# Two later layers: banded attention steps between the products of the projection tiles, norms applied behind the products, and half of the output projection inside the difference attention

## What is computed

```python
for l in range(DEPTH):
    h = rmsnorm_2(x, g_attn[l])
    proj = jnp.einsum('bsd,dc->bsc', h, w_in[l])
    qa, ka, va, qb, kb, vb = jnp.split(proj, offs, axis=-1)
    ...
    ya = windowed_gqa_sink(qa, ka, va, sink[l])
    yb = diff_attention(qb, kb, vb, lam)
    yb = rmsnorm_2(yb, subln[l]) * (1.0 - lambda_init)
    y = jnp.concatenate([ya.reshape(B, S, SWA_Q), yb.reshape(B, S, DIFF_V)], axis=-1)
    x = x + jnp.einsum('bsm,md->bsd', y, w_out[l])
    h = rmsnorm_2(x, g_ffn[l])
    gate, val = jnp.split(jnp.einsum('bsd,df->bsf', h, w_up[l]), 2, axis=-1)
    gate = centred_dwconv(gate, conv_w[l], conv_b[l])
    x = x + jnp.einsum('bsf,fd->bsd', jax.nn.silu(gate) * val, w_down[l])
```

## Time and profile before

| | |
|---|---|
| median of 3 runs | 3187.5 us (3186.05 to 3193.69) |
| the profiled execution | 3192.74 us |
| its span, first to last instruction | 3191.0 us |
| busy: TensorE, VectorE, ScalarE | 2972.4, 1523.6, 1190.8 us |
| mean granted TensorE clock | 0.972 of 2.4 GHz |
| the first later layer, from its norm to its end | 678.2 us (1830.3 to 2508.5) |
| the second | 679.5 us (2508.5 to 3188.0) |

### The profile page before, as it was taken

How to read it: one execution, slowest core, us unless ns; L and a number is a source line. 1 busy time by engine, 2 the same in 40 slices (tenths; PEclk the granted TensorE clock), 3 DMA queues, 4 the chain that set the end, 5 groups by cost and what they waited for, 6 DMA issues and landing times.

```text
span 3191.0 us, 36914 instructions
## 1 busy us (share of the span) xinstructions
PE 2972.4 (93%) x14632; PEld 2430.2 (76%) x14632; DVE 1523.6 (48%) x2217; ACT 1190.8 (37%) x1784; POOL 0.2 (0%) x4
## 2 busy tenths in 40 slices
PE   6999699999999889999999998789999997899999
PEld 4788588999999766557888776368888774478887
DVE  3121755552454444436636456855444457654343
ACT  3111543331332365334424344643233444543232
POOL 0000000000000000000000000000000000000000
PEclk9999899999999999999999999999999998999999
DMA  6665001221212111002322211012223220023223
GB/s 243 220 225 183 7 31 53 67 67 59 66 60 71 49 39 39 1 14 95 107 92 93 99 67 53 1 53 99 100 92 102 76 73 14 14 86 106 87 98 106
DMA packets 67276, 255.94 MB, mean 80 GB/s; under 512 B 7456, under 2 KB 11168, under 8 KB 66464
## 3 DMA queue, kind: packets, MB, share of 16 engines
q1 hardware_dynamic: 67104, 253.58, 23.1%
HBM read 251.46 MB, written 2.10 MB: 79 GB/s over the span
## 4 chain that ended last, share of the span: by engine, by line
PE 85%; DVE 6%; DMA 3%; ACT 3%; issue 3%; SPq 0%; DVEq 0%; ACTq 0%
PE psum L520 71%; DVE arena L1371 2%; ACT temps L1014 2%; DVE row_stats L1371 2%; DMA modulation_weights<-in_ada 2%; PE psum L837 2%; PE psum L856 1%; PE psum L834 1%; PE psum L559 1%; PE psum L977 1%; DMA arena<-in_ada_first 1%; PE psum L757 1%; PE psum L771 1%; PE psum L847 1%; DVE temps L1371 1%
## 5 line engine op out<-in xcount | busy, mean ns | idle before, releaser
L520 PE MATMUL psum<-arena_r,w_hi 128*128 128x512 f32 (+1 forms) x7640 | 2077.3, 371 | 42.3 <-DVE arena_r L1371 38.8
L520 PEld LDWEIGHTS psum<-arena_r,w_hi 128*128 128x128 f32 x7640 | 1404.0, 189 | 254.4 <-issue 78.0
L520 PE MATMUL psum<-arena_r,w_lo 128*128 128x512 f32 (+1 forms) x3820 | 1264.6, 367 | 0.0
L1371 DVE TENSOR_TENSOR w_lo<-w_raw,w_hi 128x1024 fp32r<-128x1024 f32 (+3 forms) x367 | 453.9, 1237 | 768.8 <-ACT w_hi L1014 768.7
L520 PEld LDWEIGHTS psum<-arena_r,w_lo 128*128 128x128 f32 x3820 | 709.4, 189 | 84.9
L1014 ACT ACTIVATE w_hi<-w_raw 128x1024 fp32r<-128x1024 f32 (+3 forms) x367 | 391.7, 1067 | 829.6 <-DMA w_raw<-in_weights 829.4
L1371 DVE SCALAR_TENSOR_TENSOR temps<-psum,vectors,temps 128x511 f32<-128x511 f32 x352 | 228.0, 679 | 150.4 <-ACT temps L1014 147.3
L1014 ACT ACTIVATE temps<-psum,vectors 128x512 f32<-128x512 f32 (+1 forms) x132 | 112.2, 850 | 179.8 <-PE psum L520 178.4
L1014 ACT ACTIVATE arena<-psum 128x768 f32<-128x768 f32 (+1 forms) x134 | 96.6, 727 | 155.3 <-PE psum L520 63.7
L1014 ACT ACTIVATE temps<-temps 128x512 f32<-128x512 f32 (+2 forms) x165 | 108.3, 656 | 90.6 <-DVE temps L1371 88.6
L1014 ACT ACTIVATE temps<-psum 128x512 f32<-128x512 f32 (+1 forms) x142 | 86.9, 655 | 145.6 <-PE psum L520 123.8
(11 more groups left out here) (147 smaller groups left out, 1850.9 us busy)
## 6 DMA issues: line engine op xcount, KB each, us to landing
w_raw<-in_weights SPq DMA_DIRECT2D x275, 512.0 KB, 3.2
w_raw<-in_weights SPq DMA_DIRECT2D x64, 704.0 KB, 4.0
temps<-in_ada SPq DMA_DIRECT2D x40, 512.0 KB, 3.6
modulation_weights<-in_ada SPq DMA_DIRECT2D x40, 512.0 KB, 4.4
arena<-in_ada_first SPq DMA_DIRECT2D x4, 2048.0 KB, 23.7
X<-in_xt SPq DMA_DIRECT2D x1, 3072.0 KB, 12.6
phase_constants<-in_const SPq DMA_DIRECT2D x3, 768.0 KB, 7.4
w_raw<-in_weights SPq DMA_DIRECT2D x12, 192.0 KB, 2.3
```

Of the source, the lines that this page charges most:

```text
L520: last = mm(lin_at(t, segs, slots, upper)[:, s:s + m], w[:, c], x(k, s, m), start=(k == 0 and a == 0), stop=(k == n_k - 1 and a == 2))
L1371: op(*args, **kw).then_inc(*C.out(signal))
```

## The change

Four things, in both later layers.

**The factor of the norm is applied behind the products.** The products take X times the gain, as it is (`raw_hi` by ScalarE, `raw_low` by VectorE, made while the residual is added); the sums of squares come between blocks 3 and 4 of the first tile; each result is then multiplied by 1/rms on VectorE: all 18 projection tiles (`scaled`), the 22 gate tiles, and the 22 products of gate and value.

**Banded steps inside the projection.** Tiles 9 to 17 carry two steps each, cut in between their blocks. The order of TensorE's banks changes: linear tiles have two banks instead of four, tails and rotations share bank 0, banded scores have one pair of banks, turned ones another.

**Turning by a product.** Instead of dividing the 512 or 768 exponentials by their sum and transposing, VectorE writes a diagonal matrix of the two heads' reciprocals (`SHARE`), and an ordinary fp32 product with it both turns and divides.

**Half of the output projection inside the difference attention.** The tiles of w_out are cut into two halves of 4 blocks; the first half, which needs the banded heads alone, runs as 8 tiles of 12 products between the 16 steps, and is added to X there (8 more additions). The turned blocks have one bank instead of two, and values and sum of squares share bank 2. The second half follows as 8 tiles of 12 products.

```diff
-        t += [(8, P, lambda g, l=l, c=m * P: columns(paired_rows(g["w_out_2"][l]), c)) for m in range(8)]
+        for part in range(2):
+            t += [(4, P, lambda g, l=l, r=part * 512, c=m * P: columns(paired_rows(g["w_out_2"][l])[r:r + 512], c)) for m in range(8)]
...
+        BAND = 9
+        def band_step(n):
+            return 2 * (n - BAND) if BAND <= n < 18 else None
...
+                if raw:
+                    linear(1, segs, hi, lo, "free_v", 4, progress("raw_done", 8), between=lambda k: norm_sum(segs) if k == 3 else None)
+                else:
+                    norm_sum(segs)
+                    linear(2, segs, hi, lo, "free_v", 4, progress("h_done", 8))
...
+                def tail(n):
+                    pe.wait_ge(sems["free_a"], first + n + 1)
+                    if n:
+                        taken_from(n - 1)
+                    wait(pe, C.at("rot_done", on="rope_made"))
+                    if specs[n]["kind"] == "norm":
+                        last = mm(PS[:, 0, :], blk, T[:, n % 2, 0:NX], start=True, stop=True)
+                    else:
+                        for t in range(4):
+                            last = pe.transpose(PS[:, 0, t * P:(t + 1) * P], T[:, n % 2, t * P:(t + 1) * P], ident)
+                    last.then_inc(*C.out("tail_sum"))
...
+                def rotation(n, latest):
+                    if n < 0 or specs[n].get("rope") is None:
+                        return
+                    pe.wait_ge(sems["tail_made"], tails + n + 1)
+                    taken_from(latest)
+                    wait(pe, C.at("rot_done", on="rope_made"))
+                    mm(PS[:, 0, :], CP[:, PC_ROT:PC_ROT + P], f_(specs[n]["rope"], NX), start=True, stop=True).then_inc(*C.out("rot_done"))
...
-                            last = pe.transpose(PS[:, hf, t * P:(t + 1) * P], f_(a, P), ident)
+                            last = mm(PS[:, 6 + hf, t * P:(t + 1) * P], f_(a, P), SHARE[n % 2][:, hf], start=True, stop=True)
...
+                def between(n):
+                    p = band_step(n)
+                    def at(k):
+                        if n == 0 and k == 3:
+                            sums()
+                        if p is not None:
+                            if k == 0:
+                                scores(p)
+                            if k == 2:
+                                turn(p - 1)
+                            if k == 4:
+                                values(p - 2)
+                                scores(p + 1)
+                        if n and k == (3 if p is None else 5):
+                            tail(n - 1)
+                        if p is not None:
+                            if k == 6:
+                                turn(p)
+                            if k == 7:
+                                values(p - 1)
+                        if k == 7:
+                            rotation(n - 3, n - 1)
+                    return at
...
+                ready = progress("raw_done", 8)
+                for n in range(18):
+                    linear(1, ONLY_X, raw_hi, raw_lo, "free_a", 2, ready if n == 0 else None, between(n), t0)
...
-                    if n >= 2:
-                        pe.wait_ge(sems["pt_made"], base + n - 1)
+                    if n:
+                        pe.wait_ge(sems["pt_made"], base + n)
+                    else:
+                        taken_from(17)
...
-                        last = pe.transpose(PS[:, n % 2, t * P:(t + 1) * P], f_(E2 + n % 4 * 1024 + t * P, P), ident)
+                        last = pe.transpose(PS[:, 0, t * P:(t + 1) * P], f_(E2 + n % 4 * 1024 + t * P, P), ident)
...
-                        pe.wait_ge(*C.at("od_made"))
+                        pe.wait_ge(*C.at("sub_rs"))
...
+                for m in range(8):
+                    linear(1, ONLY_X, hi2, lo2, "free_v", 2, ready if m == 0 else None,
+                           lambda k: difference(2 * m + k // 2) if k % 2 else None, t0)
...
+            def raw_low(m, gain):
+                dve.wait_ge(*C.next("raw_hi"))
+                step(stt, "raw_done", r_(RAW0 + 8 * NX + m * NX, NX), X[:, m, 0:NX], gain(m), r_(RAW0 + m * NX, NX).bitcast(F32),
+                     ALU.mult, ALU.subtract)
...
+                        if raw and part == 0:
+                            dve.wait_ge(*C.at("lin_done"))
+                            src = SCALED[i % 2]
+                            step(tt, "raw_scaled", halves(src), halves(lin_at(t, segs, 4)), RS, ALU.mult)
...
+                    if raw:
+                        step(tt, "prod_made", halves(T[:, 3, 0:NX]), halves(T[:, 3, 0:NX]), RS, ALU.mult, after=C.at("free_v"))
...
-                    step(tt, "p_made", e, e, ST[:, s + 12:s + 14].rearrange("p (h o) -> p h o", o=1).broadcast_to([P, 2, w]), ALU.mult,
-                         after=C.at("dve_own"))
+                    step(tt, "p_made", SHARE[n % 2], CF[:, C_ID:C_ID + P].rearrange("p (o q) -> p o q", o=1).broadcast_to([P, 2, P]),
+                         ST[:, s + 12:s + 14].rearrange("p (h o) -> p h o", o=1).broadcast_to([P, 2, P]), ALU.mult, after=C.at("dve_own"))
...
+                for n in range(1, 19):
+                    p = band_step(n)
+                    scaled(n - 1)
+                    if p:
+                        probs(p - 1)
+                    if p is not None and p < 16:
+                        maxima(p)
+                    if p is not None and p >= 6 and p % 4 == 2:
+                        low((p - 6) // 4)
+                    if n < 18:
+                        ahead()
+                    if n >= 2 and (specs[n - 2]["kind"] == "norm" or n < BAND + 1):
+                        tail(n - 2)
+                    if n >= 4 and specs[n - 4].get("rope") is not None:
+                        rotate(specs[n - 4]["rope"], PS[:, 0, :])
+                    if p is not None and p < 16:
+                        probs(p)
+                    if n >= BAND and specs[n - 1]["kind"] != "norm":
+                        tail(n - 1)
+                    if p is not None and p + 1 < 16:
+                        maxima(p + 1)
...
+                    if n % 2 == 0:
+                        t = ahead()
+                        dve.wait_ge(*C.at("lin_done"))
+                        x = X[:, n // 2, 0:NX]
+                        step(tt, "free_v", x, lin_at(t, ONLY_X, 2, t0), x, ALU.add)
```

267 lines of the change are left out of this document (166 added, 101 removed).

## The result

The changed kernel takes 3216.65 us (median of 4 runs, 3215.71 to 3221.45), beside 3188.2 us for the kernel before: a ratio of 1.0081, 95% interval 1.0067 to 1.0095. It is **slower by 0.8%**. The forecast of 3192.5 us was 24 us low, and its most likely case, no change, did not come; the time that came is close to the third rival's 3214 us. The first later layer now takes 691.7 us (678.2 before). Two such layers give 27.0 us, and the medians lie 28.5 apart. The spans of the two profiled executions (3215.1 us against 3191.0) differ by less, since the first later layer begins 3.0 us sooner in the second (1827.3 against 1830.3) and the one before was 5 us above its median.

What follows compares the result with a forecast made beforehand. TensorE was taken to bound the kernel (85% of the chain of waits). Per layer -15.4 - 27.4 + 10.4 + 33 + 2 + 15.4 - 15.5 = +2.5, both layers +5: 3187.5 + 5 = 3192.5 us, range 3152 to 3222.

Steps and rivals of the forecast that it cites:

- most likely case, no change: Whole kernel: large terms nearly cancel, time within 9.6 us of 3187.5; chance 0.40.
- third rival: Difference attention hides nothing and its clock sinks: 10.6 us more per layer, 3214 us; chance 0.27.
- Norms: At the norms, gaps and slow clock go while the sums stay: -15.4 us per layer.
- the remaining half: Output projection's second half: VectorE and ScalarE set 3.2 us per tile; with the net's start, -15.5 us per layer.
- the start of the net: Feed-forward net's first tile: norm sum waits 2.8 us; counted within the remaining half's -15.5 us per layer.
- Tail and rotation in one bank: Projection tiles 4 to 8: TensorE waits 4.6 us five times, plus 10 for slow clock: +33 us per layer.
- 0, if the wait were covered: Lower bound of the cost of tail and rotation sharing one bank; the upper bound was 41 us.
- first rival: Tiles 4 to 8: the wait for the rotation is covered, 33 us per layer go, 3126 us; chance 0.15.
- Turning by a product: Banded steps: 80 blocks at 0.27 us instead of a transpose's 0.14, +10.4 us per layer; keeping transposes 20.8 faster overall.
- Banded steps inside the tiles: Banded attention's 63.0 us stage goes, 35.6 us of TensorE work enters projection tiles: -27.4 us per layer.
- Difference attention: With half the output projection inside: 84.1 us against 68.7, +15.4 per layer, two thirds of the moved work not hidden.
- waits in the banded tiles: Tiles 9 to 16: rotation late by about 0.7 us in three tiles, +2 us per layer.

Runs made afterwards that it cites:

- experiment 1: The change with VectorE's w_lo subtraction moved behind tail and rotation in tiles 4 to 8: 3148.8 us, ratio 0.9861 to the kernel before.
- experiment 3: The change with probabilities turned by transposes again and VectorE dividing all of them: 3211.7 us, ratio 1.0058 to the kernel before.
- experiment 5: The change with the output projection's first half run behind the difference attention instead of inside it: 3230.0 us, ratio 1.0117 to the kernel before.
- experiment 4: The change with the difference attention's addition to X moved into the odd step, behind its probabilities: 3204.9 us, ratio 1.0033 to the kernel before.
- experiment 7: The change with the difference attention's first maximum ahead of the last tail and last banded low half: 3214.4 us, ratio 1.0076 to the kernel before.
- experiments 5 and 6: The second of these is experiment 5's kernel with turned blocks going to two banks in turn: 3229.6 us, ratio 1.0116 to the kernel before.
- the run with all orders: The change with w_lo behind tail and rotation, both additions to X moved, transposes, and first maximum ahead of last tail: 3106.0 us, ratio 0.9730 to the kernel before.
- experiment 2: The change with unread products filling TensorE's waits in tiles 4, 5, 6 and 8 and before tile 6's rotation: 3203.1 us, ratio 1.0027.

## Why the prediction was right or wrong

Per layer the forecast was +2.5 us and the measurement is +13.5.

**Norms, the remaining half, the start of the net: right.** The gaps are gone. The second half of the projection runs at 3.28 us per tile (forecast 3.2), and the norm sum of the net waits 2.45 us (2.8). From the end of the difference attention to the end of the layer it is 390.2 us, against 413.2 before: -23.0, forecast -23.4.

**Tail and rotation in one bank: right, and it decides.** Five stalls, 25.4 us (forecast 23), and 10.5 for the clock behind them (10): 35.9 where the record has 33, and experiment 1 gets back all but the 1.4 us that it leaves. One of the five isn't where I put it: the tail of tile 7 doesn't wait. In its place it is the rotation in tile 6, for 6.17 us, because VectorE itself copies the value tile's turned blocks out of the bank, behind a `w_lo` that waits for its load (1899.33, the copy at 1900.47). The bound "0, if the wait were covered" and the first rival fall.

**Turning by a product: the price was too high, its direction right.** In the change four take 0.81 us and hold the next pair up by 0.09, 0.22 each and not 0.27; against 0.14 that is 6.4 us per layer, not 10.4. What experiment 3 gets back is only 3.6. On this kernel a transpose would have been about 7 us cheaper in all and not 20.8 (by the traces; the intervals of the times overlap): the price was too high, and VectorE's larger division takes part of the rest back.

**Banded steps inside the tiles: too cheap by what the cuts cost.** Without the stalls the projection with the banded steps takes 177.4 us from its first block (experiment 1: 2.6 + 174.8). My terms without the stall give 173.8 (7.8 + 125.5 + 63.0 - 7.5 - 27.4 + 10.4 + 2), and that with a product 4 us too dear. So 7.6 us are missing. Of these 0.7 are waits for VectorE (2.7 us in that run, 2 in my terms). I had taken the banded rows from start to start in a stage of their own. Inside the tiles each place where they cut in costs more:

```profile
1960.35 0.71 PE L538 MATMUL psum<-arena_r,w_hi 128*128 128x512 f32 x2
1960.90 0.40 PE L538 MATMUL psum<-arena_r,w_lo 128*128 128x512 f32 x1
1961.22 0.67 PE L984 MATMUL psum<-arena 128*64 128x128 f32 x8
...
1965.22 0.62 PE L538 MATMUL psum<-arena_r,w_hi 128*128 128x512 f32 x2
1965.68 0.39 PE L538 MATMUL psum<-arena_r,w_lo 128*128 128x512 f32 x1
1965.91 1.50 PE L969 MATMUL psum<-temps,arena 128*128 128x128 f32 x12
```

From start to start, a pair of linear products takes 0.46 us (1965.22 to 1965.68), but 0.55 behind a turning (1960.35 to 1960.90). A single one takes 0.23 (1965.68 to 1965.91), but 0.32 ahead of values (1960.90 to 1961.22). A tile has some seven such edges, about 0.7 us, and eight tiles give 5 to 6. The two behind the turnings of each tile, 1.4 us, are already in the 0.22 above, so some 4 us are new, and 2 to 3 of the 7.6 stay unexplained. No run took the edges by themselves, so their share is worked out and not shown.

**Difference attention: the step that failed.** The record has 84.1 us, +15.4 with "two thirds of what moves in is not hidden". Measured are 89.7, +21.0 from the same 68.7. (The row of 68.7 in the earlier trace rows begins 1.9 us ahead of the first scores; from the scores themselves it is the +22.9 of experiment 5.) So nearly nothing of the 22.0 us is hidden. The mechanism was right where it was worked out: eight steps take 39.2 us (forecast 39.0), and VectorE's addition to X ahead of the normalizing holds them up (experiment 4). What went wrong are the two ends, for which the record gives a figure without a working. The first four steps took 24.4 us where the record has 20.3: VectorE does the last tail and `low` ahead of the first maximum, because the stage no longer begins with everything behind it done, and that order costs 3.1 us (experiment 7). From the last four steps on it was 26.1, not 24.8, with the last values at a clock of 0.56: 6.52 us instead of 3.70 at full clock, and 5.33 in the kernel before. Together that is 5.4 of the 5.6 us missing.

**The third rival: its total by luck.** It names the same cause, that nothing is hidden, and that nearly came true. But it puts all of its 10.6 us per layer in this stage, with 4 for the clock, and the stage is 5.6 us over my 84.1, just under the 90 us that were to show this rival. The other half of what made the total 3214 comes from the projection.

**The sum.** Measured less forecast, per layer, by the boundaries of the earlier trace rows: projection with banded steps +15.6 against +10.5, difference attention +21.0 against +15.4, the rest -23.0 against -23.4. That makes 5.1 + 5.6 + 0.4 = 11.1, which is 13.5 less 2.5 but for rounding. The 5.1 are +2.9 of stalls, -4.0 of turning, -0.7 of waits in the banded tiles and +6.9 of banded steps inside the tiles. The chances had faster and slower nearly alike and the range held the time; but the no-change case rested on large terms cancelling to within 5 us, when the two that were too small both were costs of moved work in its new surroundings.

## What to carry to other kernels

When a result is read back on a shared bank, walk the list of the engine that empties it: any operation there that waits for something issued late, here a subtraction for weights that are needed two tiles on, must stand behind what the busy engine waits for. Moving that one operation was worth 2.2%, more than the change had cost. Moved work is to be priced where it lands: at each edge with the work around it, and with what used to be finished before the stage began. And where waits can't be taken away, ask what the idle time does to the clock, since a stage can get longer with the same instructions.

## What was not expected of the hardware

The stage of the difference attention ran the same products at a clock of 1.00 in its middle in the kernel before, and at 0.89 in experiments 5 and 6, with the same waits in that middle and 3.2 us more ahead of it; that cost 3.6 us per layer. In the run with all orders, where products stand inside, the stage is at 1.00. What sets which of the two it is was not found. Filling idle TensorE with products nobody reads made the changed kernel 0.5% faster (experiment 2).
